# First attention of a two-block kernel: a tile's values multiplied ahead of the next tile's transposes

## What is computed

```python
logits = einsum('bqhc,bqkc->bqhk', qb_lat, kv_sel) + bias
logits = where((dist >= 0)[:, :, None, :], logits, -inf)
p = softmax(logits, axis=-1)
o_lat = einsum('bqhk,bqkc->bqhc', p, kv_sel)
o = einsum('bthc,hcv->bthv', o_lat, w_uv)
```

## Time and profile before

| | us |
|---|---|
| Median of 3 runs | 2332.53 (2332.31 to 2332.61) |
| The profiled execution's own time | 2331.14 |
| Its span, first to last instruction | 2329.0 |
| PE busy in the span | 2198.0 (94%) |
| DVE busy | 1763.4 (76%) |
| ACT busy | 1131.9 (49%) |
| Mean granted TensorE clock | 0.953 of full speed |

### The profile page before, as it was taken

The page is one execution under the profiler, slowest core; times in us unless marked ns, Lnnn a source line. Parts: engine busy times, 40 slices in busy tenths (PEclk is TensorE's granted clock), DMA queues, the critical chain, the costliest instruction groups (busy, mean ns, idle before and its releaser), DMA issues. The chain is left out here.

```text
span 2329.0 us, 31104 instructions
## 1 busy us (share of the span) xinstructions
PE 2198.0 (94%) x10909; PEld 1868.8 (80%) x10909; DVE 1763.4 (76%) x2938; ACT 1131.9 (49%) x1944; POOL 421.9 (18%) x417
## 2 busy tenths in 40 slices
PE   8989899998999999999999989899999999999996
PEld 5779888886877788888887979777878788888875
DVE  7699855565599987878788585573799977767897
ACT  5478655554353333335444563484563333554442
POOL 2123122213330122220001212103321122000002
PEclk9985599999999999999999999899999999999997
DMA  9025200005443333238531101002356445755422
GB/s 380 29 71 154 79 14 14 32 1 169 150 136 119 142 115 115 90 118 315 186 93 40 46 28 37 19 2 97 103 190 239 168 153 195 246 197 179 124 91 73
DMA packets 93098, 276.38 MB, mean 119 GB/s; under 512 B 11137, under 2 KB 15649, under 8 KB 89121
## 3 DMA queue, kind: packets, MB, share of 16 engines
q1 hardware_dynamic: 85472, 226.64, 29.3%
q10 hardware_dynamic: 7488, 47.98, 5.0%
HBM read 208.19 MB, written 66.39 MB: 118 GB/s over the span
## 5 line engine op out<-in xcount | busy, mean ns | idle before, releaser
L159 PE MATMUL banks<-f_hi,f_w_hi 128*128 128x512 f32 x608 | 237.8, 391 | 5.8 <-DVE f_w_lo L3914 4.4
L160 PE MATMUL banks<-f_lo,f_w_hi 128*128 128x512 f32 x608 | 237.3, 390 | 0.0
L161 PE MATMUL banks<-f_hi,f_w_lo 128*128 128x512 f32 x608 | 237.2, 390 | 0.0
L3442 ACT CAST f_w_hi<-f_raw 128x512 fp32r<-128x512 f32 x173 | 107.5, 622 | 255.3 <-PE banks L161 190.3
L2017 ACT CAST w_hi<-w_raw 128x512 fp32r<-128x512 f32 x152 | 93.8, 622 | 223.7 <-PE set L161 106.5
L159 PE MATMUL set<-gate_hi,w_hi 128*128 128x512 f32 x420 | 163.8, 390 | 1.2 <-DVE w_lo L2349 0.8
L161 PE MATMUL set<-gate_hi,w_lo 128*128 128x512 f32 x420 | 163.4, 389 | 0.0
L160 PE MATMUL set<-gate_lo,w_hi 128*128 128x512 f32 x420 | 163.4, 389 | 0.0
L159 PE MATMUL set<-b_hi,w_hi 128*128 128x512 f32 x384 | 150.3, 391 | 4.8 <-ACT work L2027 2.6
L3122 POOL TENSOR_TENSOR f_w_lo<-f_raw,f_w_hi 128x512 fp32r<-128x512 f32 x64 | 93.6, 1464 | 337.6 <-ACT f_w_hi L3442 337.6
L161 PE MATMUL set<-b_hi,w_lo 128*128 128x512 f32 x384 | 149.5, 389 | 0.0
(11 more groups left out here) (583 smaller groups left out, 6093.9 us busy)
## 6 DMA issues: line engine op xcount, KB each, us to landing
gates<-x ACTq DMA_DIRECT2D x25, 1536.0 KB, 6.0
w_raw<-in_w_ff SPq DMA_DIRECT2D x53, 512.0 KB, 3.7
gate_raw<-gates SPq DMA_DIRECT2D x105, 256.0 KB, 2.9
f_gate_raw<-gates SPq DMA_DIRECT2D x70, 256.0 KB, 2.8
ada<-in_ada_w SPq DMA_DIRECT2D x32, 512.0 KB, 3.5
f_raw<-in_f_w_v SPq DMA_DIRECT2D x26, 512.0 KB, 3.6
f_raw<-in_f_w_u SPq DMA_DIRECT2D x25, 512.0 KB, 3.8
down_raw<-in_w_ff SPq DMA_DIRECT2D x18, 512.0 KB, 5.1
```

Of the source, the lines that this page charges most:

```text
L159: nc.tensor.matmul(out, w_hi, x_hi, start=start, stop=False)
L160: nc.tensor.matmul(out, w_hi, x_lo, start=False, stop=False)
L161: return nc.tensor.matmul(out, w_lo, x_hi, start=False, stop=stop)
L3442: nc.scalar.copy(w_parts(n)[0][:, :], source(n)).then_inc(w_hi_s, 1)
```

## The change

In PE's loop over the tiles, the product with the values of tile m - 1 is issued ahead of the transposes of tile m instead of behind them. The order in step m becomes L(m + 2), V(m - 1), T(m). V(15) still follows T(15) at the end of a round. Nothing else is edited: the waits inside `turn` and `times_v` and the orders of the other engines stay as they are.

```diff
@@ -1194,9 +1194,9 @@
                 def body(i, last):
                     for m in range(TILES):
                         ahead(i, m + AHEAD, last, project, logits)
-                        turn(i, m // QT, m % QT)
                         if m:
                             times_v(i, (m - 1) // QT, (m - 1) % QT)
+                        turn(i, m // QT, m % QT)
                     times_v(i, 1, QT - 1)
```

## The result

The changed kernel takes 2339.94 us (median of 8 runs, 2338.28 to 2344.64) against 2333.05 us for the kernel before (8 runs, 2332.31 to 2336.82). The ratio is 1.003, 95% interval 1.002 to 1.0039: slower by 6.9 us, where 8 us were forecast (2340.5, range 2334.5 to 2346).

What follows compares the result with a forecast made beforehand. PE was taken to bound the attention stage, busy 219.67 of 236.00 us. 19.3 us uncovered less 11.4 us filled gave +7.9, taken as +8, on 2332.5: 2340.5 us, range 2334.5 to 2346.

Steps and rivals of the forecast that it cites:

- Filled: Where T(m) waits for DVE, V(m - 1) runs in the hole: 11.4 us filled of 19.1 us.
- Uncovered: PE's V(m) waits for ACT's copy of tile m, covered only by the logits L: 19.3 us of new holes.
- The sum: In the attention stage, 19.3 us uncovered less 11.4 us filled: +7.9 us, taken as +8 us.
- Step three: A later T(m) delays ACT's copy, exponential and normalising by up to 1.7 us but makes no others late: cost nothing.
- Holes filled, none opened: Rival: ACT's copy stays hidden as well as before, so only the 11.4 us count: 2321.1 us, chance 0.06.
- They cancel: Rival: ACT's signal takes no time and DVE is pulled ahead: +3.6 us, 2336, within 0.2%, chance 0.17.
- The clock falls: Rival: new holes bring PE's clock down at four round ends, 1.4 us each, 5.6 in all: 2346, chance 0.10.

Runs made afterwards that it cites:

- The experiment with five steps: Against the kernel before, V(m - 1) issued ahead of T(m) only in steps 1, 2, 3, 10 and 12: 2328.58 us, ratio 0.998.
- another set of 5: Against the kernel before, V(m - 1) issued ahead of T(m) only in steps 5, 6, 7, 14 and 15: 2345.38 us, ratio 1.0055.

## Why the prediction was right

The forecast was the sum of two large terms of opposite sign, and both can be read off the changed kernel. The mechanism was right. The size came out as near as it did partly by luck, since a cost that was put at nothing made up for the errors of the two terms.

**Filled.** 11.4 us were forecast. T's waits that are left are eight, 5.0 us, with 0.16 each 6.3; from 19.1 that makes 12.8 us filled. The term was 1.4 too small, by the shortest V's: ahead of T(1) 3.2 us stay where I had 3.95 (in the rounds 2 and 3 V(0) takes 0.37 us off its wait, from 1.28 to 0.91, where I had counted 0.2 from the pitch of its two matmuls), ahead of T(10) 1.5 where I had 2.0, and T(2) keeps nothing of its 0.2.

**Uncovered.** 19.3 us were forecast in 21 holes. Measured are 21 waits and 15.5 us; with 0.16 each that is 18.9. The single ones are close: behind T(14) 0.64 + 0.16 = 0.80 against 0.80, behind T(15) 1.10 + 0.16 = 1.26 against 1.34. The signal from ACT to PE takes 0.04 and 0.06 us in the rows above, not the 0.13 that I had borrowed from DVE. That explains the holes with no logits in them, which came out 0.08 short. The others came out as forecast because of a second error the other way: behind six transposes the logits start 0.57 us after T's start (383.23 to 383.80 in the changed kernel), where I had 0.65 (399.39 to 400.04), from V behind T.

**The sum.** 18.9 - 12.8 = 6.1 us from the waits, 1.8 less than forecast, both terms erring to the same side. That the stage itself grew by 6.1 to 6.5 us is no confirmation: at the same clock the change costs 7.4 to 8.0. The rest, about 0.4 us a round, lies in no wait. In the second round the holes grew from 4.65 to 5.83 us, 1.18 more, and the round by 1.60. Step three put the cost of waking PE at nothing, with as many holes closed as opened. But V behind logits or a hole takes longer from its start to what follows than V behind T: 14 matmuls go from 418.18 to 419.85, 1.67 us, against 384.92 to 386.40, 1.48. Over the second round V's groups take 1.9 us more by this count, and T's, now behind V, 1.5 less. 6.1 and four times 0.4 make 7.7, next to the forecast of 7.9; the runs say 6.9, within 4.7 and 9.1.

**Nothing else was made late.** Step three said that a later T does not delay what hangs on it. With T moved in 15 of 16 steps PE has no new wait for DVE, and T(6) has lost its own. The later exponentials are to be seen one engine further on, where DVE's inverse now waits for them five times, 2.9 us, instead of once, 0.5 us; DVE had that time to spare.

The experiment with five steps found the reverse effect, which step three did not treat: a filled wait lets PE arrive sooner, and the next tile then waits for DVE. In the changed kernel T(11) has no such wait.

**The rivals.** "Holes filled, none opened" falls with the 21 waits. "They cancel" had a right part in it (the signal takes 0.05 us, not 0.13), but its +3.6 us lie below the interval, which begins at 0.2%, where that case was to end. "The clock falls" did not happen: 1.00 over the 239 us that hold the 21 new holes of up to 1.3 us. The swing that the Trainium skill, "TensorE: Matmul & The Clock Gate", section "A second HAM failure mode: psum-queue depth-cycling", tells of for frequent short idle gaps between groups of matmuls did not come with these. The stretch at 0.50 that seven of the eleven profiles have near the start of the stage is there in the kernel before too, and no run here shows what sets it.

## What to carry to other kernels

When an engine waits at one instruction, moving another ahead of it fills the wait, but the moved one was standing somewhere: list what it had covered there before counting the gain. Where two engines hand one buffer back and forth (here `turned`, written by PE and emptied by ACT), something as long as the copy must stand between the write and the first use, on every step, the shortest tile and the end of the loop included. The exchange paid in a set of 5 of the 15 steps and cost in another set of 5; choosing them per step, and carrying the last piece of a loop's body into its next pass, beat both kernels.

When a sum of waits agrees with the measured difference, look at whether the two profiles had the same clock. Rounds that repeat the same work at full clock are the better measure, and they showed here a cost that stands in no wait.

## What was not expected of the hardware

The same program's stages ahead of the attention ended 4.9 us apart in two profiles, with no edit, and single runs spread over 0.4%. A difference of a few microseconds in a span of 2300 is therefore better read from the stage that the edit touches than from two profiles' totals.

Even the stage was not the same ground twice. A stretch of some 3.4 us at half clock in its first round is there in some profiles and missing in others, with the same order of instructions, and is worth 1.5 us, a fifth of what the change costs.

ACT's copy and PE's next instruction lie 0.04 to 0.06 us apart where PE was waiting; DVE's normalising and PE's transposes lie 0.13 us apart.
